# Mixer A scores on one core: keys' high and low parts in the two partition halves, queries twice, two 128-row matmuls for three 64-row ones

## The reference, cut to what matters

```
def diff_attention(q, k, v, lam):
    scale = 1.0 / math.sqrt(DK_A)          # DK_A = 64
    def attend(qb):
        s = jnp.einsum('bqhcd,bshcd->bhcqs', qb, k).astype(jnp.float32) * scale
        p = jax.nn.softmax(s, axis=-1)
        p = p[:, :, 0] - lam[None, :, None, None] * p[:, :, 1]
        return jnp.einsum('bhqs,bshe->bqhe', p.astype(v.dtype), v)
    return sweep_query_blocks(attend, q)
```

## Time and profile before

| | |
|---|---|
| time, median of 3 runs | 1397.82 us |
| span of the profiled execution | 1395.5 us |
| PE busy | 1341.7 us, 7399 matmuls |
| PEld busy | 1035.0 us |
| DVE busy | 719.3 us |
| ACT busy | 615.7 us |
| POOL busy | 216.8 us |
| DMA | 156.59 MB, mean 112 GB/s |
| PE clock in all 40 slices | 9 of 10 or more of full speed |

### The profile page before, as it was taken

The page is one execution under the profiler, slowest core; times in us unless marked ns, Lnnn a source line. Parts: engine busy times, 40 slices in busy tenths (PEclk is TensorE's granted clock), DMA queues, the critical chain, the costliest instruction groups (busy, mean ns, idle before and its releaser), DMA issues.

```text
span 1395.5 us, 19039 instructions
## 1 busy us (share of the span) xinstructions
PE 1341.7 (96%) x7399; PEld 1035.0 (74%) x7399; DVE 719.3 (52%) x1155; ACT 615.7 (44%) x1297; POOL 216.8 (16%) x374
## 2 busy tenths in 40 slices
PE   2799999999999999999999999999999999999996
PEld 1466666888888888768687776868777686788885
DVE  1444614747566575555555555554555665533243
ACT  2322312555546455454454545445455654422123
POOL 2000200302020030212212121221212321200001
PEclk9999999999999999999999999999999999999999
DMA  9999882112112121212112121211213331333234
GB/s 307 357 352 291 325 267 74 61 46 80 47 53 73 46 87 38 81 50 74 53 52 76 46 75 53 74 53 50 78 46 102 110 112 46 121 136 128 78 134 159
DMA packets 144218, 156.59 MB, mean 112 GB/s; under 512 B 8008, under 2 KB 122792, under 8 KB 143360
## 3 DMA queue, kind: packets, MB, share of 16 engines
q1 hardware_dynamic: 137232, 132.19, 29.4%
q0 software_dynamic: 6896, 23.17, 5.0%
HBM read 144.18 MB, written 11.16 MB: 111 GB/s over the span
## 4 chain that ended last, share of the span: by engine, by line
PE 91%; DVE 3%; DMA 3%; SPq 2%; ACT 1%; issue 0%; ACTq 0%; POOL 0%; DVEq 0%
PE z_ps L540 24%; PE z_ps L541 21%; PE z_ps L542 21%; PE ring L635 5%; PE ring L702 5%; PE ring L540 5%; PE ring L542 3%; PE ring L541 3%; PE ring L704 2%; PE ring L560 2%; DMA x_sb<-in_x_sample_dram 1%; SPq L453 1%; PE ring L728 1%; DMA ada_raw<-in_w_ada_dram 1%; DMA w_raw<-in_w_in_dram 1%; PE ring L583 1%
## 5 line engine op out<-in xcount | busy, mean ns | idle before, releaser
L540 PE MATMUL z_ps<-w_hi,xt_hi 128*128 128x512 f32 x1360 | 578.4, 425 | 2.5 <-DVE xt_lo L1225 1.0
L541 PE MATMUL z_ps<-w_lo,xt_hi 128*128 128x512 f32 x1360 | 532.9, 392 | 0.0
L542 PE MATMUL z_ps<-w_hi,xt_lo 128*128 128x512 f32 x1360 | 532.9, 392 | 0.0
L540 PEld LDWEIGHTS z_ps<-w_hi,xt_hi 128*128 128x128 f32 x1360 | 255.8, 188 | 93.9 <-issue 47.0
L1081 DVE TENSOR_TENSOR w_lo<-w_raw,w_hi 128x512 fp32r<-128x512 f32 x272 | 191.4, 706 | 244.2 <-ACT w_hi L778 242.1
L778 ACT ACTIVATE w_hi<-w_raw 128x512 fp32r<-128x512 f32 x272 | 170.4, 628 | 318.7 <-PE z_ps L542 305.1
L542 PEld LDWEIGHTS z_ps<-w_hi,xt_lo 128*128 128x128 f32 x1360 | 255.5, 188 | 57.4
L541 PEld LDWEIGHTS z_ps<-w_lo,xt_hi 128*128 128x128 f32 x1360 | 257.3, 189 | 33.2
L1161 DVE TENSOR_REDUCE small<-s_sb 128x2 f32<-128x1536 f32 (+1 forms) x60 | 88.9, 1482 | 105.3 <-ACT s_sb L778 105.3
L778 ACT ACTIVATE s_sb<-ring 128x256 f32<-128x256 f32 (+2 forms) x144 | 67.3, 468 | 124.4 <-PE ring L542 123.5
L877 ACT ACTIVATE s_sb<-s_sb,small 128x768 f32<-128x768 f32 (+1 forms) x120 | 98.0, 820 | 5.3 <-DVE small L1161 5.3
(11 more groups left out here) (141 smaller groups left out, 1275.9 us busy)
## 6 DMA issues: line engine op xcount, KB each, us to landing
w_raw<-in_w_in_dram SPq DMA_DIRECT2D x208, 256.0 KB, 3.1
ada_raw<-in_w_ada_dram SPq DMA_DIRECT2D x64, 512.0 KB, 8.8
w_raw<-in_w_out_dram SPq DMA_DIRECT2D x64, 256.0 KB, 3.4
gate_pt<-in_w_ada_dram SPq DMA_DIRECT2D x12, 512.0 KB, 6.4
gate_sg<-in_w_ada_dram SPq DMA_DIRECT2D x12, 512.0 KB, 6.3
o_spill<-row_st POOLq DMA_DIRECT2D x14, 320.0 KB, 3.1
row_st<-o_spill POOLq DMA_DIRECT2D x14, 320.0 KB, 3.3
x_sb<-in_x_sample_dram SPq DMA_DIRECT2D x4, 1024.0 KB, 13.7
```

The source lines that it names most:

```text
L540: pe.matmul(out, hi_l, hi_r, start=start, stop=False)
L541: pe.matmul(out, hi_l, lo_r, start=False, stop=False)
L542: return pe.matmul(out, lo_l, hi_r, start=False, stop=stop)
```

## The change: what it does, and the diff

Each component's q is written twice side by side (`q_two`), so that its transpose has the same 64 rows in both partition halves; `q_hi` and `q_lo` then hold [q_c over q_c] for each component c. Of k only one tile per component is left: `k_hi[:, c]` has the high part of component c in the half where the transpose put it, and its low part in the other half; for component 0 high is in partitions 0 to 63, for component 1 in 64 to 127. VectorE writes the low part across, from one half to the other. One 128-row matmul of q_hi with this tile gives high x high + high x low, one of q_lo gives low x high + low x low. A part of mixer A has two matmuls of 128 rows instead of three of 64. The QK step has five banks instead of three, its 12 transposes become 17, its four copies and four subtractions become eight and eight, and the first score part waits for five banks. `q_two` lies over `k_lo`, which mixer A no longer uses. `half` of before is renamed `minus_half`. Mixer B is unchanged.

```diff
-        return 4 if g == "KV" else 3
+        return 4 if g == "KV" else 5 if g == "D" else 3
...
     k_hi, e = place("k_hi", [P, 2, NKEY + P], F32R, e)
+    q_two, _ = place("q_two", [P, TILES, 2, 2, DK_A], F32, e)
     k_lo, e = place("k_lo", [P, 2, NKEY + P], F32R, e)
...
 
             n = TURN[("QK", a, 0)]
             g = group_kind(a)
             S, C = LAT * P, PAST * P
+            every, keys = slice(0, P), slice(S, S + C + P)
             if g == "D":
-                return [(n, 0, S, q_hi[:, 0, 0:S], q_lo[:, 0, 0:S], True),
-                        (n + 1, 0, S, k_hi[:, 0, 0:S], k_lo[:, 0, 0:S], True),
-                        (n + 2, 0, C + P, k_hi[:, 0, S:S + C + P], k_lo[:, 0, S:S + C + P], False),
-                        (n + 2, C + P, P, q_hi[:, 0, S:S + P], q_lo[:, 0, S:S + P], True)]
+                lat = [(n + c, every, 0, S, q_hi[:, c, 0:S], q_lo[:, c, 0:S], True) for c in range(2)]
+                k_lat = [(n + 2, half[c], 0, S, k_hi[half[c], c, 0:S], k_hi[half[1 - c], c, 0:S], c == 1)
+                         for c in range(2)]
+                k_rest = [(n + 3, half[c], 0, C + P, k_hi[half[c], c, keys], k_hi[half[1 - c], c, keys], False)
+                          for c in range(2)]
+                prompt = [(n + 3 + c, every, (C + P) * (1 - c), P, q_hi[:, c, S:S + P], q_lo[:, c, S:S + P], True)
+                          for c in range(2)]
+                return lat + k_lat + k_rest + prompt
             if g == "KV":
-                return [(n + c, 0, S, k_hi[:, c, 0:S], k_lo[:, c, 0:S], True) for c in range(2)] + \
-                    [(n + 2 + c, 0, C + P, k_hi[:, c, S:S + C + P], k_lo[:, c, S:S + C + P], True) for c in range(2)]
-            return [(n + c, 0, S, q_hi[:, c, 0:S], q_lo[:, c, 0:S], True) for c in range(2)] + \
-                [(n + 2, P * c, P, q_hi[:, c, S:S + P], q_lo[:, c, S:S + P], c == 1) for c in range(2)]
+                return [(n + c, every, 0, S, k_hi[:, c, 0:S], k_lo[:, c, 0:S], True) for c in range(2)] + \
+                    [(n + 2 + c, every, 0, C + P, k_hi[:, c, keys], k_lo[:, c, keys], True) for c in range(2)]
+            return [(n + c, every, 0, S, q_hi[:, c, 0:S], q_lo[:, c, 0:S], True) for c in range(2)] + \
+                [(n + 2, every, P * c, P, q_hi[:, c, S:S + P], q_lo[:, c, S:S + P], c == 1) for c in range(2)]
...
+            def q_twice(bank, col, t, c_):
+
+                return transpose(bank, col, q_two[:, t, c_].rearrange("p u d -> p (u d)"))
+
+            def step_qk_d(bank, part):
+
+                if part < 2:
+                    for t in range(1, TILES):
+                        ins = q_twice(bank, P * (t - 1), t, part)
+                elif part == 2:
+                    for t in range(1, TILES):
+                        ins = transpose(bank, P * (t - 1), zs[:, t, DH:2 * DH])
+                elif part == 3:
+                    for j in range(PAST):
+                        transpose(bank, P * j, kv_raw[:, 0, j, 0:DH])
+                    transpose(bank, P * PAST, zs[:, 0, DH:2 * DH])
+                    ins = q_twice(bank, P * (PAST + 1), 0, 0)
+                else:
+                    ins = q_twice(bank, 0, 0, 1)
+                return ins
+
             def step_qk(a, part):
                 n = TURN[("QK", a, 0)] + part
...
                 if t == 0 and part == 0:
-                    for u in range(3):
+                    for u in range(banks_of("QK", a, 0)):
                         wait_free(pe, TURN[("QK", a, 0)] + u)
                 if t == 0:
                     c_, k0, kn, q0 = part, NKEY, P, LAT * P
                 else:
                     (c_, u), q0 = divmod(part, 2), P * (t - 1)
                     k0, kn = ((0, 512), (512, NKEY - 512))[u]
+                out = claim(n)[:, 0:kn]
                 if group_kind(a) == "D":
-                    rows, qh, kh = slice(DK_A * c_, DK_A * (c_ + 1)), 0, 0
+                    pe.matmul(out, q_hi[:, c_, q0:q0 + P], k_hi[:, c_, k0:k0 + kn], start=True, stop=False)
+                    ins = pe.matmul(out, q_lo[:, c_, q0:q0 + P], k_hi[:, c_, k0:k0 + kn], start=False, stop=True)
                 else:
-                    rows, qh, kh = slice(0, P), c_, (a - G_IT) // 2
-                filled(split_matmul(claim(n)[:, 0:kn], q_hi[rows, qh, q0:q0 + P], q_lo[rows, qh, q0:q0 + P],
-                                    k_hi[rows, kh, k0:k0 + kn], k_lo[rows, kh, k0:k0 + kn]), n)
+                    kh = (a - G_IT) // 2
+                    ins = split_matmul(out, q_hi[:, c_, q0:q0 + P], q_lo[:, c_, q0:q0 + P], k_hi[:, kh, k0:k0 + kn],
+                                       k_lo[:, kh, k0:k0 + kn])
+                filled(ins, n)
...
             def qk_his(a):
-                for n, col, w, hi, _, _ in qk_parts(a):
+                for n, rows, col, w, hi, _, _ in qk_parts(a):
                     wait_full(act, n)
-                    copy(hi, RB(n)[:, col:col + w]).then_inc(qk_hi_done, 1)
+                    copy(hi, RB(n)[rows, col:col + w]).then_inc(qk_hi_done, 1)
...
                 link(dve.tensor_tensor(tmp[3], x2, cos, ALU.mult))
+                if g == "D":
+                    for u in range(2):
+                        dve.tensor_tensor(q_two[:, 1:, :, u, 0:half_d], tmp[0][:, :, 0:2], tmp[1][:, :, 0:2], ALU.subtract)
+                        dve.tensor_tensor(q_two[:, 1:, :, u, half_d:], tmp[2][:, :, 0:2], tmp[3][:, :, 0:2], ALU.add)
+                    dve.tensor_copy(q_two[:, 0], zs[:, 0, 0:DH].rearrange("p (c d) -> p c d", c=2).unsqueeze(2)
+                                    .broadcast_to([P, 2, 2, DK_A]))
+                    x1, x2, tmp = x1[:, :, 2:4], x2[:, :, 2:4], [b[:, :, 2:4] for b in tmp]
                 link(dve.tensor_tensor(x1, tmp[0], tmp[1], ALU.subtract))
                 dve.tensor_tensor(x2, tmp[2], tmp[3], ALU.add).then_inc(qk_ready, 1)
...
             def qk_los(a):
                 q0 = sum(QKP[:a])
                 turns = [part[0] for part in qk_parts(a)]
-                for n, col, w, hi, lo, last in qk_parts(a):
+                for n, rows, col, w, hi, lo, last in qk_parts(a):
 
                     dve.wait_ge(qk_hi_done, q0 + max(i for i, m in enumerate(turns) if m == n) + 1)
-                    ins = dve.tensor_tensor(lo, RB(n)[:, col:col + w], hi.bitcast(F32), ALU.subtract)
+                    ins = dve.tensor_tensor(lo, RB(n)[rows, col:col + w], hi.bitcast(F32), ALU.subtract)
                     if last:
                         ins.then_inc(free_sem(n), 1)
 
```

More of the change, by code:

```diff
@@ L281, in build @@
     stat = new("stat", [P, 2, 16])
-    half = new("half", [P, 16])
+    minus_half = new("minus_half", [P, 16])
     ssq = new("ssq", [P, TILES, 4])
@@ L370, in build @@
         N_VH = [1 if group_kind(a) == "D" else 2 if group_kind(a) == "KV" else 0 for a in range(OUT_IT)]
+        half = [slice(0, DK_A), slice(DK_A, P)]
         def qk_parts(a):
@@ L644, in step_qk @@
                 bank = claim(n)
-                if part < 2:
+                if g == "D":
+                    ins = step_qk_d(bank, part)
+                elif part < 2:
                     for t in range(1, TILES):
@@ L651, in step_qk @@
                 else:
-                    c_ = part - 2 if g == "KV" else 0
+                    c_ = part - 2
                     for j in range(PAST):
                         transpose(bank, P * j, kv_raw[:, 0, j, DH * c_:DH * (c_ + 1)])
-                    if g == "KV":
-                        ins = transpose(bank, P * PAST, zs[:, 0, DH * c_:DH * (c_ + 1)])
-                    else:
-                        transpose(bank, P * PAST, zs[:, 0, DH:2 * DH])
-                        ins = transpose(bank, P * PAST + P, zs[:, 0, 0:DH])
+                    ins = transpose(bank, P * PAST, zs[:, 0, DH * c_:DH * (c_ + 1)])
                 filled(ins, n)
@@ L1362, in _ @@
             link = linker(pool, pool_chain)
-            link(pool.memset(half[:, :], -0.5))
+            link(pool.memset(minus_half[:, :], -0.5))
             pool.memset(ident[:, :], 0.0).then_inc(id_set, 1)
@@ L1378, in inv_root @@
                 link(pool.tensor_scalar(out, in_, 1.0 / mean_of, EPS, ALU.mult, ALU.add))
-                return pool.tensor_tensor(out, out, half[:, 0:n], ALU.pow)
+                return pool.tensor_tensor(out, out, minus_half[:, 0:n], ALU.pow)
             for t in range(TILES):
@@ L1469, in load_out_operands @@
                     pool.wait_ge(g_ready, G_DONE[OUT_IT - 1])
-                    wait_free(pool, TURN[("QK", OUT_IT - 1, 0)] + 2)
+                    wait_free(pool, TURN[("QK", OUT_IT - 1, 0)] + banks_of("QK", OUT_IT - 1, 0) - 1)
                 cols = slice(NCOL * cc, NCOL * (cc + 1))
@@ L1492, in _ @@
                                 link(pool.tensor_scalar(stat[:, 1, 0:10], stat[:, 0, 0:10], DH * EPS, None, ALU.add))
-                                pool.tensor_tensor(stat[:, 1, 0:10], stat[:, 1, 0:10], half[:, 0:10],
```

(3 more changed lines are left out.)

## The result

The changed kernel takes 1345.28 us (median; 1344.95 to 1345.86), the one before 1397.65 us in the same session: a ratio of 0.9627 (0.9616 to 0.9639), 52.4 us less. Forecast were 1333.4 us in a range of 1320 to 1347. Sign, place and matmul terms were right; the cost of the new wait was twice what I said.

A forecast was written before the change was run, and what follows sets the result against it. TensorE's own stream was taken to bound the kernel: -81 us for score matmuls, +4.6 for transposes and +12 for the new wait make -64.4, so 1333.4 us, with 1320 to 1347 to hold 8 of 10.

The forecast's parts named there:

- matmul terms: TensorE in mixer A: score parts save 81 us, five more transposes a head add 4.6 us.
- new wait: First score part of each head, step s=4, waits for ScalarE's and VectorE's splits: 1.5 us a head, 12 us in all.
- The bound: TensorE's own stream sets the end; an insertion costs what it pushes the projection matmuls apart, not its duration.
- Third matmul and row switch: Mixer A score parts without the third matmul and the 64-row borders: 10.1 us a head saved, 81 us in all.
- The packing rule: Skill's rule that matmuls on different row tiles can run in parallel; as a rival 1426 us, chance 0.01.
- The transposes and the q writes: Five more transposes a head cost 0.57 us, 4.6 us in all; doubled q writes, some 1.2 us, cost nothing.
- Later score parts: Score steps behind the first part of a head: nothing is late, since ScalarE empties a bank in 0.6 us.
- long-stall rival: First score part of each head: half-partition writes are dear, stall 30 us in all, 1351 us; chance 0.1.
- hidden-stall rival: First score part of each head: ScalarE and VectorE keep up, only matmul terms count, 1321 us; chance 0.14.

The follow-up runs named there:

- late_s0: Changed kernel with the two 128-wide prompt score parts behind projection tiles 3 and 4 of step s=4 instead of 0 and 1: 1322.83 us.
- three_128: Kernel before, with all three score matmuls of mixer A kept but on 128 rows instead of 64: 1339.97 us.
- whole_rows: Changed kernel with the copies and subtractions of k on all 128 partitions instead of 64, same number and width: 1334.27 us.
- early_and_late: Changed kernel, q and k transposes and splits at s=2 for the first six heads, prompt score parts behind tiles 3 and 4 for all: 1321.47 us.
- same_half: Changed kernel with the low parts of k written to the partition half they are read from, in the other component's tile: 1345.55 us.
- more_subs_5: Kernel before, with five more 384-wide VectorE subtractions ahead of the last q_lo subtraction of each mixer A head: 1428.67 us.
- mid_s0: Changed kernel with the two prompt score parts behind tiles 1 and 2 of step s=4 instead of 0 and 1: 1333.66 us.

## Why the prediction was right, and where it was off

In short: the matmul terms and the place of the new wait were right, and its cost was not. 1345.28 us lies outside the 1326 to 1344 us that I gave the forecast itself, and inside 1320 to 1347 only because the range was stretched towards the rivals. That it held was luck.

**The bound.** Right: TensorE's stream set the end, and the pushing apart of the projection matmuls was the measure of an insertion. Busy durations would have misled: by their sums the 512-wide part has 1.27 us before and 0.78 after, a saving of 0.49 us, where the stream gained 0.64.

**Third matmul and row switch.** Forecast 81 us, shown apart as 25.4 and 57.9. late_s0, in which no wait for the split is left, lies 75.1 us below the kernel before; 81 less the 4.6 us of the transposes was 76.4. Its heads 2 to 6 are 81.63 - 72.10 = 9.53 us shorter, to the hundredth the forecast 10.1 - 0.57; the seventh lacks 0.8 of it.

**The packing rule.** It spoke against the change and would have made it 1426 us. Nothing ran beside anything before, and giving up 64 rows gained 57.9 us in three_128. What the Trainium skill says beside it (TensorEngine Tiling (Array Packing), Key Properties), that changing the tiling mode drains TensorE, agrees with the 0.32 us gaps of the earlier trace rows and with their absence in three_128. The rule that was of use was this one.

**The transposes and the q writes.** Right. q_two costs nothing on TensorE's path beyond 0.57 us a head; VectorE's copy of the prompt's q takes 0.73 us, more than I allowed, and is hidden.

**The new wait.** Place, releaser and chain were right. Its size is the term that was off: 12 us forecast (1.5 us a head), about 23 us measured (603.1 - 580.0, the sum of the heads less that of late_s0). Two things were missing. First, I took the overlap of operations back to back from rows on 128 partitions, and the operations on the halves of k have none. Counted from ScalarE's first copy of k, VectorE starts 0.12 us later than in whole_rows (881.57 - 880.33 against 876.21 - 875.10), needs 0.33 us more for its four subtractions, and the next one follows 0.09 us later. With all 128 partitions the wait is 1.57 us, close to my 1.5. The wake-up is 884.87 - 884.62 = 0.25 us; my 0.15 had no row. That makes 2.13 us a head, 17 us. Second, I priced a wait at its own length. At four heads it also drew a fall of the clock, 4 x 1.6 = 6.4 us; the prediction has no term for it. The sentence that the wait "costs in full" was too weak: it costs more than itself.

**Later score parts.** I wrote that nothing behind the wait is late, and named PE idle before later score parts as a sign of being wrong. Two such waits are there, 0.3 us each, in the seventh head alone. The error is under 1 us.

**The range.** The long-stall rival (1351 us) came close in size for a wrong reason: the half-wide subtractions are not dearer, 0.69 us as ever. The hidden-stall rival (1321 us) is where late_s0 and early_and_late lie, since they move what the wait is for; in the changed kernel itself the stall was not hidden.

## What to carry to other kernels

Where matmuls on 64 rows stand one by one among matmuls on 128 rows, filling the rows is worth more than saving a matmul; look at the spacing at the borders, not at durations. When a change adds serial work ahead of a fixed reader, move the reader or the work in the same edit: here three tiles of cover gave 22.5 us for an order of two small parts. Price a wait of TensorE at its length, and at 2 us of idle add the falls of its clock (1.6 us each here, behind half of the waits or more; none behind 1.4 us, and nothing was measured between), and test it by putting the same wait into the old kernel.

## What the runs showed of the hardware that I had not expected

- The clock can be granted at half after a wait of 2 us. With 1.96 to 2.0 us of idle it fell behind four of eight waits in the changed kernel and in same_half, and behind seven of eight in more_subs_5; with 1.4 us (whole_rows) and 1.3 us (mid_s0) behind none. A fall of 3.4 us costs 1.6 us, one of 6.8 us (more_subs_5, first and last head) about 3 us. What decides between equal waits stays open. It is not which head it is: same_half has the same waits and the falls in other heads.
- ScalarE and VectorE operations back to back on alternating partition halves lack the overlap of about 0.1 us that operations on all 128 partitions have, and so does the 128-partition operation behind them; whether the change of half or the narrower operation in front is the reason stays open. The duration of one doesn't depend on 64 or 128 partitions (0.69 us at 512 columns on VectorE), and VectorE writes across the halves for nothing (1345.28 us against 1345.55 without).
- Matmuls on 64 rows between matmuls on 128 rows cost about 0.2 us at each border, and the weight load at the border doesn't run ahead of its matmul (913.70 for both).
